# Five plain gate and up pairs for six in a block kernel on one core

## The chip, the cores and the metric

The kernel runs on one core of a Trainium2 chip. The metric is the device time of one launch in microseconds, the median of three runs.

## What is computed

A transformer block on x of 512 tokens by 2048 channels, in float32: a mixer of two head groups (forgetting attention and a gated linear recurrence), and behind it a gated feed-forward part of 6144 hidden channels with a short causal convolution.

```
def conv_gated_mlp(h, w_gate, w_up, conv_ffn_w, conv_ffn_b, w_down):
    g = causal_dwconv(h @ w_gate, conv_ffn_w, conv_ffn_b)
    return (jax.nn.gelu(g) * (h @ w_up)) @ w_down
...
        x = x + rmsnorm(y, norm_mix_post[l])
        h = rmsnorm(x, norm_ffn_pre[l])
        y = conv_gated_mlp(h, w_gate[l], w_up[l], conv_ffn_w[l], conv_ffn_b[l], w_down[l])
        x = x + rmsnorm(y, norm_ffn_post[l])
```

## The kernel before

Data lies channel-major: tiles of 128 channels by 512 tokens. Each float32 operand of a matmul is taken as a high part, rounded to fp32r by ScalarE, and a low part, the rest, formed by VectorE; a product is three matmuls (high by high, high by low, low by high). A matmul here always has 128 x 128 weights and 256 columns.

The feed-forward part has 48 hidden tiles (`FT`), each a gate tile and an up tile that give one tile of h; I call them a pair. The first `PLAIN` = 6 pairs are done plainly. A half tile is one unit of weights (128 x 1024): 8 channel tiles by 2 halves of the tokens by 3 matmuls, 48 in all, and a pair has four units. The first two pairs are computed together, in units 0 to 7, channel tile by channel tile as x1 becomes ready; units 8 to 23 then follow two by two with `tile`. The other `NS` = 42 pairs are done with seven products in place of eight, in the manner of Strassen. A fast product has 24 matmuls. Its right operands are quadrants of the activations (P00, P01, P10, P11, in act_hi and act_lo) and the sums T0 to T3, in tsum. Its left operands are A11, S2, S1, S3, A12, S4 and A22, made from the four weight units of a pair: S1 and S3 by a load with a second, accumulating load on the POOL queue behind it (L722, L727), S2 and S4 by VectorE.

Units and products are named by number in the text: split u is the split of unit u, counted from N_FF.

All five engines run written-out programs that are kept in step by semaphores, so the order in the code is the order on the chip.

- ScalarE: `split(u, s)` waits until the unit has landed in raw[s] and unit u - 2 is used, and writes the high part (L775). `root(5, ...)` takes the root of the channel sum of x1 squared (L780). `gain_x1(k)` scales two tiles of x1. `t_hi(k)` writes the high part of T for channel tile k (L1063). `last_tap` and `gelu_gate` are the convolution's last tap and the gelu.
- VectorE: `split` (L1226), `invert_root` (a reciprocal, L1237), `gate_in(j)` (bank times rms into gb, L1724), `taps(j)` (L1728, L1730), `up_tile(j)` (h_out = bank times cv, L1769), `t_form(k)` (four instructions, L1795 to L1799, into sq), `t_lo(k)` (L1804). T for the down projection is made from h: after an odd pair `t_of_pair(m)` (L1744 to L1747), after the next even one `t3_of_pair(m)` (L1755). sq is the one buffer of `t_form`, so t_form(k + 1) waits for t_split of k.
- SP: loads unit u once split u - 2 is done (L508). Behind the last plain unit it loads for the first fast pair S1 (L539), A11 (L548, waits for the last but one split), S3's first part (L556, behind it), A12 (L565) and A22.
- POOL queue: the stores of T of pair m (`store_pair(m)`: to_stored is L659, te_stored L661, then L664, L665; `store_t3(m)`: L670) and the accumulating loads `add_to_s1`, `add_to_s3`, in the order of this code:

```
            for j in range(PLAIN - 2):
                store_after(j)
            add_to_s1(0)
            add_to_s3(0)
            store_after(PLAIN - 2)
            add_to_s1(1)
```

`store_after(3)` is `store_pair(1)`, and `t3_of_pair(m)` on VectorE waits for it, as it overwrites half of h_out 1:

```
                dve.wait_ge(to_stored, 16 * m + 16)
                dve.wait_ge(tq_ready, m + 1)
```

TensorE waits for a split ahead of each unit and product, and for all eight t_lo ahead of the fast products. The high part of the first fast product's weights waits for all eight t_form, since its place (w_2) is memory that x1 held.

Of the kernel before, what the change touches and what calls it, by code (L numbers as in the profile page):

```python
# [29 lines left out]
P = 128  # L30
# [19 lines left out]
U_OUT = U_MIX + PER_PAIR * NP  # L50
U_FF = U_OUT + 2 * KT
U_DOWN = U_FF + 4 * FT
PLAIN = 6
NS = FT - PLAIN
U_FAST = U_FF + 4 * PLAIN
U_HID = U_FAST + 7 * NS
# [114 lines left out]
def block_kernel(nc, xT, par_d, weights, gate_w, out):  # L171
# [5 lines left out]
    with ExitStack() as ctx:  # L177
# [232 lines left out]
        def t_free_after(c, n):  # L410
# [7 lines left out]
        t2_flat = tsum_f32[:, 2].rearrange("p a k n -> p (a k n)")  # L418
        Y_TILES = [gb[:, 0:S], cv[:], up[:], sq[:, 0]] + [t2_flat[:, S * t:S * t + S] for t in range(8)] + [
            h_out[:, 0], h_out[:, 1], y_rest[:], rms[:]]  # L420
        ADD_BANKS = (banks[2], banks[3], banks[4], banks[5], banks[7], banks[6])
        Y_STAGE = ((rms[:], y_rest[:]), (h_out[:, 0], h_out[:, 1]))


# [345 lines left out]
        def _(act):  # L770
            def split(u, s, more=MORE):

                act.wait_ge(raw_landed[s], (u - s) * 8 + (16 + more[s]))
                at_least(act, unit_used, u - 1)
                act.activation(w_hi[s], k_tiles(raw[:, s]), ACT.Copy).then_inc(hi_done, 1)  # L775

            def root(n, bank, dst, width=D):

                act.wait_ge(sum_done, n)
                act.activation(dst, bank[:], ACT.Sqrt, scale=1.0 / width, bias=eps[:, 0:1]).then_inc(std_done, 1)  # L780
# [296 lines left out]
            gain_x1(2)  # L1077
            gain_x1(3)
            split(N_FF + 11, 1)
            root(5, SB[2], std)  # L1080
            gain_x1(4)
            split(N_FF + 12, 0)
            last_tap(0)
            gain_x1(5)
            split(N_FF + 13, 1)
            gelu_gate(0)
            last_tap(1)
            split(N_FF + 14, 0)
            gelu_gate(1)
            t_hi(0)  # L1090
            last_tap(2)
            split(N_FF + 15, 1)
            gelu_gate(2)
            gain_x1(6)
            last_tap(3)
            split(N_FF + 16, 0)
            t_hi(1)
            gelu_gate(3)
            gain_x1(7)
            split(N_FF + 17, 1)  # L1100
            t_hi(2)
            split(N_FF + 18, 0)
            t_hi(3)
            split(N_FF + 19, 1)
            last_tap(4)
            t_hi(4)
            split(N_FF + 20, 0)
            t_hi(5)
            gelu_gate(4)
            split(N_FF + 21, 1)  # L1110
            t_hi(6)
            split(N_FF + 22, 0)
            t_hi(7)
            split(N_FF + 23, 1)

            def product_hi(i, n):

# [102 lines left out]
        def _(dve):  # L1220
# [585 lines left out]
            def open_used(j, part):  # L1806
                return N_FF + (OPEN if j < 2 else 4 * j + 2 + 2 * part)

            split(N_FF + 11, 1)
            invert_root(5, rms[:], std, 4)  # L1810
            dve.scalar_tensor_tensor(out=acc[:], in0=std, scalar=EPS * D / P, in1=std, op0=ALU.mult, op1=ALU.mult)
            chain(dve.memset(gb[:, 0:2], 0.0))
            split(N_FF + 12, 0)
            gate_in(0, SB[0], open_used(0, 0))
            taps(0)
            split(N_FF + 13, 1)
            up_tile(0, SB[1], open_used(0, 1))
            t_after(0)
            gate_in(1, PT[0], open_used(1, 0))
            t_form(0)  # L1820
            taps(1)
            split(N_FF + 14, 0)
            up_tile(1, PT[1], open_used(1, 1))
            t_after(1)
            gate_in(2, PJ[0], open_used(2, 0))
            t_lo(0)
            taps(2)
            split(N_FF + 15, 1)
            up_tile(2, PJ[1], open_used(2, 1))
            t_after(2)  # L1830
            gate_in(3, PT[2], open_used(3, 0))
            t_form(1)
            taps(3)
            split(N_FF + 16, 0)
            t_lo(1)
            t_form(2)
            split(N_FF + 17, 1)
            up_tile(3, SB[2], open_used(3, 1))
            t_after(3)
            t_lo(2)  # L1840
            t_form(3)
            split(N_FF + 18, 0)
            t_lo(3)
            t_form(4)
            split(N_FF + 19, 1)
            gate_in(4, PJ[0], open_used(4, 0))
            t_lo(4)
            t_form(5)
            taps(4)
            split(N_FF + 20, 0)  # L1850
            t_lo(5)
            t_form(6)
            split(N_FF + 21, 1)
            up_tile(4, PJ[1], open_used(4, 1))
            t_after(4)
            t_lo(6)
            t_form(7)
            split(N_FF + 22, 0)
            t_lo(7)
            split(N_FF + 23, 1)  # L1860

            def product_lo(i, n):

# [147 lines left out]
                at_least(dve, yacc_added, k)  # L2011
                dve.tensor_tensor(acc[:], acc[:], sq[:, 1], ALU.add).then_inc(yacc_added, 1)

            gate_in(PLAIN - 1, PT[0], N_FAST - 2)
            form_s2(0)
            lo(0, 0)
            taps(PLAIN - 1)
# [1 line left out]
            for i in range(NF):  # L2019
                j = PLAIN + i  # L2020
                square = 2 * (i - 1 - NS - 2 * PAIRS_OUT)
                if i:
                    c21_of(i - 1)
                lo(i, 2)
                if i == NS + 1:
                    t_after(FT)
                if square >= 0:
                    add_y_square(square)
                if 0 < i <= NS:
                    taps(j - 1)  # L2030
                lo(i, 3)
                first_of_b(i)
                form_s4(i)
                lo(i, 4)
                if i == 0:
                    up_tile(PLAIN - 1, PT[1], N_FAST)
                elif i <= NS:
                    fast_h(j - 1, i - 1)
                if i <= NS:
                    t_after(j - 1)  # L2040
                if square >= 0:
                    add_y_square(square + 1)
# [39 lines left out]
        def _(pe):  # L2082
# [355 lines left out]
            tile(N_FF + 16, PJ[0])  # L2438
            pe.wait_ge(h_done, 3)
            tile(N_FF + 18, PJ[1])  # L2440
            pe.wait_ge(gate_taken, 2)
            tile(N_FF + 20, PT[0])
            pe.wait_ge(h_done, 2)
            tile(N_FF + 22, PT[1])

            def fast_product(i, n, region, start):

# [29 lines left out]
                else:  # L2477
                    unsplit_product(i, n, region, start)

            pe.wait_ge(t_split, UK)  # L2480
            for i in range(NF):
                a, b, c = [bank[:, 0:HS] for bank in banks[2 + 3 * (i % 2):5 + 3 * (i % 2)]]
                if i > 1:
                    pe.wait_ge(c11_taken, i - 1)
                else:
                    pe.wait_ge(gate_taken, (1, PLAIN)[i])
                one_product(i, 0, a, True)
                if i > 1:
# [109 lines left out]
```

## Time and profile before

| what | value |
|---|---|
| median of three runs | 2143.8 us (2143.32 to 2144.41) |
| the profiled execution | 2143.2 us |
| its span in the trace | 2141.4 us |
| TensorE (PE) busy | 2124.1 us, 99% |
| VectorE (DVE) busy | 1684.1 us, 79% |
| ScalarE (ACT) busy | 1023.3 us, 48% |
| TensorE's granted clock | 0.999 of full speed |

Busy times are sums over the whole span. Matmuls overlap one another and their ends are modelled, so TensorE's work is read from the starts and counts of its matmuls, not from busy time.

### The profile page before, as it was taken

What the parts mean: (1) busy time and instruction counts of PE and PEld (TensorE: products, weight loads), DVE (VectorE), ACT (ScalarE), POOL (GpSimd) and SP (SyncE); (2) the same over time, 40 slices, a digit from 0 to 9 for tenths busy, and PEclk for the clock granted to TensorE, in tenths of its full rate; (3) what the DMA queues carried; (4) which work ended last, traced back from release to release, by engine and by line L of the source; (5) the groups of instructions that cost most, each with busy time, mean ns of one, the idle gap of its engine ahead of it and who ended that gap; (6) DMA issues with size and microseconds to landing.
All of it is one profiled execution on the core that took longest, in us unless ns stands there. A gap on an engine that the chain in (4) does not pass through costs nothing.

```text
span 2141.4 us, 44252 instructions
## 1 busy us (share of the span) xinstructions
PE 2124.1 (99%) x18238; PEld 2093.2 (98%) x18238; DVE 1684.1 (79%) x2297; ACT 1023.3 (48%) x1287; POOL 342.5 (16%) x428
## 2 busy tenths in 40 slices
PE   9999999999999999999999999999999999999998
PEld 8999999999999999999999999999999999999997
DVE  7777777778855877888888888888887867767876
ACT  6555554456322554444444444444444545445543
POOL 0222222222100001212112121121211001012002
PEclk9999999999999999999999999999999999999999
DMA  5788988888543435887887878788888658679645
GB/s 178 163 195 208 209 190 204 200 186 193 155 130 99 153 112 171 233 217 212 220 217 220 225 208 221 214 224 222 230 219 277 193 155 290 177 190 278 204 138 187
DMA packets 238754, 423.84 MB, mean 198 GB/s; under 512 B 17008, under 2 KB 151792, under 8 KB 237312
## 3 DMA queue, kind: packets, MB, share of 16 engines
q1 hardware_dynamic: 147776, 256.84, 36.2%
q0 software_dynamic: 88224, 159.97, 36.0%
q10 hardware_dynamic: 2592, 4.72, 0.6%
q8 instruction: 120, 1.97, 0.4%
q14 instruction: 42, 0.34, 0.0%
HBM read 382.64 MB, written 89.16 MB: 220 GB/s over the span
## 4 chain that ended last, share of the span: by engine, by line
PE 93%; DVE 3%; issue 1%; ACT 1%; DMA 1%; POOL 1%; POOLq 0%; DVEq 0%; ACTq 0%
PE bank L2086 29%; PE bank L2088 29%; PE bank L2087 29%; PE bank L2470 2%; PE bank L2165 1%; PE bank L2178 1%; DVE w_all L1226 1%; DMA act_lo_f<-t_spill 1%; PE bank L2190 0%; PE bank L2189 0%; ACT act_hi L1144 0%; ACT w_all L775 0%; PE bank L2250 0%; DMA t_spill<-h_out 0%; DVE tsum L1804 0%
## 5 line engine op out<-in xcount | busy, mean ns | idle before, releaser
L2086 PE MATMUL bank<-act_hi,w_all 128*128 128x256 f32 x3272 | 909.9, 278 | 5.2 <-DVE w_all L1226 2.5
L2088 PE MATMUL bank<-act_hi,w_all 128*128 128x256 f32 x3272 | 903.9, 276 | 0.0
L2087 PE MATMUL bank<-act_lo,w_all 128*128 128x256 f32 x3272 | 903.8, 276 | 0.0
L2086 PEld LDWEIGHTS bank<-act_hi,w_all 128*128 128x128 f32 x3272 | 614.2, 188 | 11.4 <-issue 4.0
L2087 PEld LDWEIGHTS bank<-act_lo,w_all 128*128 128x128 f32 x3272 | 614.3, 188 | 0.7 <-issue 0.2
L2088 PEld LDWEIGHTS bank<-act_hi,w_all 128*128 128x128 f32 x3272 | 614.3, 188 | 0.0
L2086 PE MATMUL bank<-tsum,w_all 128*128 128x256 f32 x1280 | 353.5, 276 | 0.0
L2088 PE MATMUL bank<-tsum,w_all 128*128 128x256 f32 x1280 | 353.3, 276 | 0.0
L2087 PE MATMUL bank<-tsum,w_all 128*128 128x256 f32 x1280 | 353.3, 276 | 0.0
L1138 ACT ACTIVATE w_all<-raw_s 128x1024 fp32r<-128x1024 f32 x172 | 182.9, 1063 | 242.8 <-PE bank L2088 222.1
L1226 DVE TENSOR_TENSOR w_all<-raw,w_all 128x1024 fp32r<-128x1024 f32 x134 | 164.1, 1225 | 133.6 <-ACT w_all L775 131.9
L1869 DVE TENSOR_TENSOR w_all<-raw_s,w_all 128x1024 fp32r<-128x1024 f32 x172 | 210.6, 1225 | 68.9 <-ACT w_all L1138 67.6
L2087 PEld LDWEIGHTS bank<-tsum,w_all 128*128 128x128 f32 x1280 | 240.2, 188 | 0.0
L2086 PEld LDWEIGHTS bank<-tsum,w_all 128*128 128x128 f32 x1280 | 240.2, 188 | 0.0
L2088 PEld LDWEIGHTS bank<-tsum,w_all 128*128 128x128 f32 x1280 | 240.2, 188 | 0.0
L775 ACT ACTIVATE w_all<-raw 128x1024 fp32r<-128x1024 f32 x133 | 140.7, 1058 | 159.1 <-PE bank L2088 156.8
L2086 PE MATMUL bank<-tsum,w 128*128 128x256 f32 x656 | 181.7, 277 | 0.2 <-DVE pu L1942 0.2
L2087 PE MATMUL bank<-tsum,w 128*128 128x256 f32 x656 | 181.2, 276 | 0.0
L2088 PE MATMUL bank<-tsum,w 128*128 128x256 f32 x656 | 181.1, 276 | 0.0
L2086 PE MATMUL bank<-act_hi,w 128*128 128x256 f32 x568 | 157.3, 277 | 0.0
L2088 PE MATMUL bank<-act_hi,w 128*128 128x256 f32 x568 | 156.8, 276 | 0.0
L2087 PE MATMUL bank<-act_lo,w 128*128 128x256 f32 x568 | 156.8, 276 | 0.0
(401 smaller groups left out, 3524.2 us busy)
## 6 DMA issues: line engine op xcount, KB each, us to landing
raw<-weights SPq DMA_DIRECT2D x262, 512.0 KB, 4.2
w_sums<-weights POOLq DMA_DIRECT2D x96, 512.0 KB, 6.9
raw_s<-weights SPq DMA_DIRECT2D x84, 512.0 KB, 5.4
raw_s<-weights POOLq DMA_DIRECT2D x84, 512.0 KB, 5.7
raw_a<-weights SPq DMA_DIRECT2D x66, 512.0 KB, 5.6
raw_s<-w_sums SPq DMA_DIRECT2D x48, 512.0 KB, 5.2
t_spill<-h_out POOLq DMA_DIRECT2D x48, 256.0 KB, 3.7
act_lo_f<-t_spill POOLq DMA_DIRECT2D x11, 1024.0 KB, 10.0
```

Of the source, the lines that this page charges most:

```text
L775: act.activation(w_hi[s], k_tiles(raw[:, s]), ACT.Copy).then_inc(hi_done, 1)
L1138: act.activation(w_slot(q)[0], k_tiles(RAW_OF[n](i)), ACT.Copy).then_inc(hi_done, 1)
L1226: dve.tensor_tensor(w_lo[s], k_tiles(raw[:, s]), word(w_hi[s]), ALU.subtract).then_inc(split_done, 1)
L1869: dve.tensor_tensor(lo, k_tiles(RAW_OF[n](i)), word(hi), ALU.subtract).then_inc(split_done, 1)
L2086: pe.matmul(dst, ah, bh, start=start, stop=False, skip_group_check=goes_on)
L2087: pe.matmul(dst, ah, bl, start=False, stop=False, skip_group_check=goes_on)
L2088: return pe.matmul(dst, al, bh, start=False, stop=stop, skip_group_check=goes_on)
L2165: last[e] = pe.matmul(dst, q, k, start=t == 0, stop=t == 2)
L2178: last = pe.transpose(dst, sm[:, c:c + P], ident[:])
L2470: last = pe.matmul(region, w[:, k // 2, k % 2], summed[:, k], start=start and k == 0, stop=k == UK - 1, skip_group_check=not start)
```

## The change

`PLAIN` is 5 in place of 6, so the plain pairs end with unit 19 and there are 43 fast pairs. The last plain pair is now number 4, in PJ[0] and PJ[1], handled at the start of the fast loop (gate_in, taps, up_tile). In the opening T 0 and T 1 are formed ahead of the reciprocal, splits, T steps and convolution steps are reordered, the root is written to acc instead of sq, and t3_of_pair(1), which stood behind up_tile(4) and ahead of t_lo(6), stands between t_lo(6) and t_form(7), ahead of up_tile(4). The wait for t_split stands behind the first fast product. The lines that name `PLAIN` elsewhere aren't in the diff, but change with it: the POOL code above now runs store_after(0 to 2), the two additions, store_after(3).

```
-PLAIN = 6
+PLAIN = 5
...
-        ADD_BANKS = (banks[2], banks[3], banks[4], banks[5], banks[7], banks[6])
+        ADD_BANKS = (banks[5], banks[6], banks[7], banks[2], banks[4], banks[3])
...
             split(N_FF + 11, 1)
-            root(5, SB[2], std)
+            t_hi(0)
+            split(N_FF + 12, 0)
+            root(5, SB[2], acc[:])
             gain_x1(4)
-            split(N_FF + 12, 0)
-            last_tap(0)
+            t_hi(1)
             gain_x1(5)
             split(N_FF + 13, 1)
+            last_tap(0)
+            split(N_FF + 14, 0)
             gelu_gate(0)
+            t_hi(2)
...
             def gate_in(j, bank, used):
                 dve.wait_ge(unit_used, used)
+                at_least(dve, conv_done, j)
...
             split(N_FF + 11, 1)
-            invert_root(5, rms[:], std, 4)
-            dve.scalar_tensor_tensor(out=acc[:], in0=std, scalar=EPS * D / P, in1=std, op0=ALU.mult, op1=ALU.mult)
+            t_form(0)
+            t_lo(0)
+            t_form(1)
+            split(N_FF + 12, 0)
+            invert_root(5, rms[:], acc[:], 4)
             chain(dve.memset(gb[:, 0:2], 0.0))
...
             split(N_FF + 18, 0)
-            t_lo(3)
-            t_form(4)
-            split(N_FF + 19, 1)
-            gate_in(4, PJ[0], open_used(4, 0))
             t_lo(4)
             t_form(5)
-            taps(4)
-            split(N_FF + 20, 0)
+            split(N_FF + 19, 1)
             t_lo(5)
             t_form(6)
-            split(N_FF + 21, 1)
-            up_tile(4, PJ[1], open_used(4, 1))
-            t_after(4)
             t_lo(6)
+            t3_of_pair(1)
             t_form(7)
-            split(N_FF + 22, 0)
             t_lo(7)
-            split(N_FF + 23, 1)
+            dve.scalar_tensor_tensor(out=acc[:], in0=acc[:], scalar=EPS * D / P, in1=acc[:], op0=ALU.mult, op1=ALU.mult)
...
-            gate_in(PLAIN - 1, PT[0], N_FAST - 2)
+            gate_in(PLAIN - 1, PJ[0], N_FAST - 2)
...
-                if i <= NS:
+                if 0 < i <= NS:
                     t_after(j - 1)
...
-            pe.wait_ge(gate_taken, 2)
-            tile(N_FF + 20, PT[0])
-            pe.wait_ge(h_done, 2)
-            tile(N_FF + 22, PT[1])
...
-            pe.wait_ge(t_split, UK)
             for i in range(NF):
...
+                if i == 0:
+                    pe.wait_ge(t_split, UK)
                 one_product(i, 1, b, True)
```

**VectorE around the reciprocal.** Before, from split 11 (L1226) to the taps of pair 0:

```order
L1226 TENSOR_TENSOR w_all<-raw,w_all 128x4x2x128
L1237 RECIPROCAL rms<-sq 128x512
L1811 SCALAR_TENSOR_TENSOR acc<-sq 128x512
L1812 MEMSET gb 128x2
L1226 TENSOR_TENSOR w_all<-raw,w_all 128x4x2x128
L1724 TENSOR_TENSOR gb<-bank,rms 128x512
L1728 SCALAR_TENSOR_TENSOR cv<-gb,par,cv 128x512
L1730 SCALAR_TENSOR_TENSOR cv<-gb,par,cv 128x512
```

With the change, where line numbers are 5 or 6 lower (L1220 is the split, L1231 the reciprocal, L1790 to L1794 form T, L1799 its low part):

```order
L1220 TENSOR_TENSOR w_all<-raw,w_all 128x4x2x128
L1790 TENSOR_TENSOR sq<-x 128x256
L1791 TENSOR_TENSOR sq<-x 128x256
L1792 SCALAR_TENSOR_TENSOR sq<-x,sq 128x256
L1794 SCALAR_TENSOR_TENSOR sq<-sq,x 128x256
L1799 TENSOR_TENSOR tsum<-sq,tsum 128x4x256
L1790 TENSOR_TENSOR sq<-x 128x256
L1791 TENSOR_TENSOR sq<-x 128x256
L1792 SCALAR_TENSOR_TENSOR sq<-x,sq 128x256
L1794 SCALAR_TENSOR_TENSOR sq<-sq,x 128x256
L1220 TENSOR_TENSOR w_all<-raw,w_all 128x4x2x128
L1231 RECIPROCAL rms<-acc 128x512
```

Two T steps and one low part moved ahead of the reciprocal, and split 12 too.

**VectorE at the end of the plain pairs.** Before, from t_lo(6) to split 23, gate_in(5), S2 and the low part of the first fast product (L1879, L1869), with the taps behind it:

```order
L1804 TENSOR_TENSOR tsum<-sq,tsum 128x4x256
L1795 TENSOR_TENSOR sq<-x 128x256
L1796 TENSOR_TENSOR sq<-x 128x256
L1797 SCALAR_TENSOR_TENSOR sq<-x,sq 128x256
L1799 SCALAR_TENSOR_TENSOR sq<-sq,x 128x256
L1226 TENSOR_TENSOR w_all<-raw,w_all 128x4x2x128
L1804 TENSOR_TENSOR tsum<-sq,tsum 128x4x256
L1226 TENSOR_TENSOR w_all<-raw,w_all 128x4x2x128
L1724 TENSOR_TENSOR gb<-bank,rms 128x512
L1879 TENSOR_TENSOR raw_s<-raw_s,raw 128x1024
L1869 TENSOR_TENSOR w<-raw,w 128x1024
```

With the change, from t_lo(6) over t3_of_pair(1) (L1750), t_form(7), t_lo(7), the moved acc (L1848) and gate_in(4) (L1719) to S2 (L1867) and the low part of the first fast product (L1857):

```order
L1799 TENSOR_TENSOR tsum<-sq,tsum 128x4x256
L1750 SCALAR_TENSOR_TENSOR h_out<-pu,h_out 128x256
L1790 TENSOR_TENSOR sq<-x 128x256
L1791 TENSOR_TENSOR sq<-x 128x256
L1792 SCALAR_TENSOR_TENSOR sq<-x,sq 128x256
L1794 SCALAR_TENSOR_TENSOR sq<-sq,x 128x256
L1799 TENSOR_TENSOR tsum<-sq,tsum 128x4x256
L1848 SCALAR_TENSOR_TENSOR acc<-acc 128x512
L1719 TENSOR_TENSOR gb<-bank,rms 128x512
L1867 TENSOR_TENSOR raw_s<-raw_s,raw 128x1024
L1857 TENSOR_TENSOR w<-raw,w 128x1024
```

t3_of_pair(1) now stands ahead of T 7, and between T 7 and the first fast product no split of a plain unit is left.

**The POOL queue, from the end of the stores of pair 0 on.** Before, with buffer numbers (the first two rows end T of pair 0, L659 to L665 are pair 1, then come the accumulating loads and store_t3(1)):

```order
L665 DMA t_spill<-pu 128x256
L670 DMA t_spill<-h_out 128x256
L659 DMA t_spill<-h_out 128x2x256
L661 DMA t_spill<-h_out 128x2x256
L664 DMA t_spill<-p1 128x256
L665 DMA t_spill<-pu 128x256
L722 DMA raw_s1<-weights 128x1024
L727 DMA raw_s3<-weights 128x1024
L670 DMA t_spill<-h_out 128x256
L722 DMA raw_s1<-weights 128x1024
```

With the change, with the same line numbers:

```order
L665 DMA t_spill<-pu 128x256
L670 DMA t_spill<-h_out 128x256
L722 DMA raw_s1<-weights 128x1024
L727 DMA raw_s3<-weights 128x1024
L659 DMA t_spill<-h_out 128x2x256
L661 DMA t_spill<-h_out 128x2x256
L664 DMA t_spill<-p1 128x256
L665 DMA t_spill<-pu 128x256
L722 DMA raw_s1<-weights 128x1024
L670 DMA t_spill<-h_out 128x256
```

The two accumulating loads of the first fast pair (L722, L727) moved from behind the four stores of pair 1 (L659 to L665) to ahead of them.

## Rows read from the trace of the kernel before

**Rows 1.** The page: the span, and busy time by engine
```profile
span 2141.4 us, 44252 instructions
...
PE 2124.1 (99%) x18238; PEld 2093.2 (98%) x18238; DVE 1684.1 (79%) x2297; ACT 1023.3 (48%) x1287; POOL 342.5 (16%) x428
```

**Rows 2.** Busy time by stretch: PE, PEld, DVE, ACT, POOL, PEclk, DMA share, GB/s
```profile
900.00:1600.00 700.00, 700.00 (x6179) 700.00 (x6178) 599.69 (x771) 329.27 (x368) 122.33 (x165) 1.00 0.82 220
```

**Rows 3.** TensorE's timeline: start us, us, what [idle before it, releaser]
```profile
768.73 0.28 PE L2086 MATMUL bank<-act_hi,w_all 128*128 128x256 f32 x1
...
775.14 0.28 PE L2087 MATMUL bank<-act_lo,w_all 128*128 128x256 f32 x1
...
805.36 0.36 PE L2086 MATMUL bank<-act_hi,w_all 128*128 128x256 f32 x1 [0.94 <-DVE w_all L1226]
...
849.47 0.28 PE L2086 MATMUL bank<-act_hi,w 128*128 128x256 f32 x1
```

**Rows 4.** VectorE's timeline, 770 to 836
```profile
770.08 1.23 DVE L1226 TENSOR_TENSOR w_all<-raw,w_all 128x1024 fp32r<-128x1024 f32 x1 [0.64 <-ACT w_all L775]
775.95 3.35 DVE L1237 RECIPROCAL rms<-sq 128x512 f32<-128x512 f32 x1 [4.64 <-ACT sq L780]
...
792.36 0.68 DVE L1769 TENSOR_TENSOR h_out<-bank,cv 128x512 f32<-128x512 f32 x1
793.08 0.42 DVE L1744 TENSOR_TENSOR p<-h_out 128x256 f32<-128x256 f32 x1
...
794.22 0.68 DVE L1724 TENSOR_TENSOR gb<-bank,rms 128x512 f32<-128x512 f32 x1
...
799.41 0.69 DVE L1769 TENSOR_TENSOR h_out<-bank,cv 128x512 f32<-128x512 f32 x1 [0.79 <-DMA t_spill<-h_out]
800.02 0.41 DVE L1755 SCALAR_TENSOR_TENSOR h_out<-pu,h_out 128x256 f32<-128x256 f32 x1
800.35 0.68 DVE L1724 TENSOR_TENSOR gb<-bank,rms 128x512 f32<-128x512 f32 x1
800.95 0.42 DVE L1795 TENSOR_TENSOR sq<-x 128x256 f32<-128x256 f32 x1
...
802.54 0.74 DVE L1728 SCALAR_TENSOR_TENSOR cv<-gb,par,cv 128x512 f32<-128x512 f32 x1
...
803.99 1.22 DVE L1226 TENSOR_TENSOR w_all<-raw,w_all 128x1024 fp32r<-128x1024 f32 x1
805.13 1.22 DVE L1804 TENSOR_TENSOR tsum<-sq,tsum 128x1024 fp32r<-128x1024 f32 x1
...
835.32 1.22 DVE L1226 TENSOR_TENSOR w_all<-raw,w_all 128x1024 fp32r<-128x1024 f32 x1
```

**Rows 5.** ScalarE's timeline, the high part of T for one k
```profile
808.16 1.07 ACT L1063 ACTIVATE tsum<-sq 128x1024 fp32r<-128x1024 f32 x1 [1.24 <-DVE sq L1799]
```

**Rows 6.** Timeline of the POOL queue's DMA issues near 842
```profile
842.42 0.87 POOL L727 DMA_DIRECT2D raw_s<-weights  x1 [4.58 <-DMA raw_s<-weights]
842.98 0.88 POOL L670 DMA_DIRECT2D t_spill<-h_out  x1
```

**Rows 7.** DMA issues of 793.3 to 793.4, last column us to landing
```profile
t_spill<-h_out POOLq DMA_DIRECT2D x1, 256.0 KB, 3.6
```

**Rows 8.** DMA issues of 842.9 to 843.0
```profile
raw_s<-weights POOLq DMA_DIRECT2D x1, 512.0 KB, 8.9
t_spill<-h_out POOLq DMA_DIRECT2D x1, 128.0 KB, 9.1
```

**Rows 9.** DMA issues of 800.7 to 800.8
```profile
t_spill<-h_out POOLq DMA_DIRECT2D x1, 128.0 KB, 2.2
```

**Rows 10.** Busy time by stretch, 707 to 713, columns as in rows 2
```profile
707.00:709.00 2.00, 1.72 (x15) 1.63 (x15) 1.67 (x3) 1.25 (x3) 0.00 (x0) 1.00 0.00 0
709.00:711.00 2.00, 1.84 (x7) 1.38 (x6) 0.91 (x4) 0.00 (x0) 0.00 (x0) 0.55 0.41 105
711.00:713.00 2.00, 2.00 (x4) 0.69 (x3) 1.72 (x5) 0.51 (x1) 0.00 (x0) 0.60 0.46 161
```

More of the change, by code:

```diff
@@ L1079, in _ @@
             split(N_FF + 11, 1)
-            root(5, SB[2], std)
+            t_hi(0)
+            split(N_FF + 12, 0)
+            root(5, SB[2], acc[:])
             gain_x1(4)
-            split(N_FF + 12, 0)
-            last_tap(0)
+            t_hi(1)
             gain_x1(5)
             split(N_FF + 13, 1)
+            last_tap(0)
+            split(N_FF + 14, 0)
             gelu_gate(0)
+            t_hi(2)
             last_tap(1)
-            split(N_FF + 14, 0)
+            split(N_FF + 15, 1)
             gelu_gate(1)
-            t_hi(0)
             last_tap(2)
-            split(N_FF + 15, 1)
+            gain_x1(6)
+            split(N_FF + 16, 0)
             gelu_gate(2)
-            gain_x1(6)
             last_tap(3)
-            split(N_FF + 16, 0)
-            t_hi(1)
+            split(N_FF + 17, 1)
+            t_hi(3)
             gelu_gate(3)
             gain_x1(7)
-            split(N_FF + 17, 1)
-            t_hi(2)
             split(N_FF + 18, 0)
-            t_hi(3)
+            t_hi(4)
             split(N_FF + 19, 1)
-            last_tap(4)
-            t_hi(4)
-            split(N_FF + 20, 0)
             t_hi(5)
-            gelu_gate(4)
-            split(N_FF + 21, 1)
             t_hi(6)
-            split(N_FF + 22, 0)
             t_hi(7)
-            split(N_FF + 23, 1)
             def product_hi(i, n):
@@ L1809, in _ @@
             split(N_FF + 11, 1)
-            invert_root(5, rms[:], std, 4)
-            dve.scalar_tensor_tensor(out=acc[:], in0=std, scalar=EPS * D / P, in1=std, op0=ALU.mult, op1=ALU.mult)
+            t_form(0)
[3 more added lines that the diff above has]
+            invert_root(5, rms[:], acc[:], 4)
             chain(dve.memset(gb[:, 0:2], 0.0))
-            split(N_FF + 12, 0)
             gate_in(0, SB[0], open_used(0, 0))
+            split(N_FF + 13, 1)
@@ L1815, in _ @@
             taps(0)
-            split(N_FF + 13, 1)
+            t_lo(1)
+            gate_in(1, PT[0], open_used(1, 0))
+            t_form(2)
+            split(N_FF + 14, 0)
             up_tile(0, SB[1], open_used(0, 1))
             t_after(0)
-            gate_in(1, PT[0], open_used(1, 0))
-            t_form(0)
+            t_lo(2)
             taps(1)
-            split(N_FF + 14, 0)
+            split(N_FF + 15, 1)
+            gate_in(2, PJ[0], open_used(2, 0))
             up_tile(1, PT[1], open_used(1, 1))
@@ L1824, in _ @@
             t_after(1)
-            gate_in(2, PJ[0], open_used(2, 0))
-            t_lo(0)
             taps(2)
-            split(N_FF + 15, 1)
+            split(N_FF + 16, 0)
+            gate_in(3, PT[2], open_used(3, 0))
             up_tile(2, PJ[1], open_used(2, 1))
             t_after(2)
-            gate_in(3, PT[2], open_used(3, 0))
-            t_form(1)
+            t_form(3)
             taps(3)
-            split(N_FF + 16, 0)
-            t_lo(1)
-            t_form(2)
             split(N_FF + 17, 1)
+            t_lo(3)
@@ L1838, in _ @@
             up_tile(3, SB[2], open_used(3, 1))
             t_after(3)
-            t_lo(2)
-            t_form(3)
+            t_form(4)
             split(N_FF + 18, 0)
-            t_lo(3)
-            t_form(4)
-            split(N_FF + 19, 1)
-            gate_in(4, PJ[0], open_used(4, 0))
             t_lo(4)
             t_form(5)
-            taps(4)
-            split(N_FF + 20, 0)
+            split(N_FF + 19, 1)
             t_lo(5)
             t_form(6)
-            split(N_FF + 21, 1)
@@ L1854, in _ @@
-            up_tile(4, PJ[1], open_used(4, 1))
-            t_after(4)
             t_lo(6)
+            t3_of_pair(1)
             t_form(7)
-            split(N_FF + 22, 0)
             t_lo(7)
-            split(N_FF + 23, 1)
+            dve.scalar_tensor_tensor(out=acc[:], in0=acc[:], scalar=EPS * D / P, in1=acc[:], op0=ALU.mult, op1=ALU.mult)
             def product_lo(i, n):
@@ L2035, in _ @@
                 if i == 0:
-                    up_tile(PLAIN - 1, PT[1], N_FAST)
+                    up_tile(PLAIN - 1, PJ[1], N_FAST)
                 elif i <= NS:
                     fast_h(j - 1, i - 1)
-                if i <= NS:
+                if 0 < i <= NS:
                     t_after(j - 1)
@@ L2485, in _ @@
                 else:
-                    pe.wait_ge(gate_taken, (1, PLAIN)[i])
+                    pe.wait_ge(gate_taken, (1, 2)[i])
                 one_product(i, 0, a, True)
@@ L2490, in _ @@
                 else:
-                    pe.wait_ge(h_done, (1, PLAIN)[i])
+                    pe.wait_ge(h_done, (1, 2)[i])
+                if i == 0:
+                    pe.wait_ge(t_split, UK)
                 one_product(i, 1, b, True)
```

## The prediction

> **What bounds the kernel now.** I read the page first. TensorE is busy for 2124.1 of 2141.4 us [rows 1], so only two things can shorten the run: fewer matmuls, or shorter holes between them. One number prices the matmuls. Between 900 and 1600 us, 6179 of them start in 700 us, 0.1133 us each, at a granted clock of 1.00 [rows 2]. A half tile of a plain pair (I call it a unit) is 48 matmuls, 5.44 us; a product of a fast pair is 24, 2.72 us.
>
> Next I read TensorE's timeline where plain pairs end and fast ones begin, because the diff acts there. Count units from the first gate and up weights, so that the change's last plain unit is 19 and the present one's is 23. Unit 10 starts at 768.73 and unit 11's second matmul at 775.14. The first fast product starts at 849.47 [rows 3]. From 775.14 to there are 13 units less one matmul, 623 x 0.1133 = 70.6 us, but 74.3 us pass. So 3.7 us are holes; the row at 805.36 is the largest of them, and the releaser is VectorE's low part of a weight split (L1226) [rows 3]. TensorE waits for VectorE here.
>
> Last I read VectorE's timeline for what each step costs, from one start to the next [rows 4]: split 1.14 (803.99 to 805.13), forming T for one k 1.60 (four instructions, 800.95 to 802.54), its low part 1.14 (the same shape as a split), gate 0.60, up 0.60, both taps 1.45, reciprocal about 3.4, t_of_pair 1.13, t3_of_pair 0.33. A T buffer is reused: T of k+1 waits until the low part of k is done, and the low part waits for ScalarE's high part, 1.07 us [rows 5]. A T step with nothing to fill that wait is about 4.1 us. Before the reciprocal VectorE is idle for 4.64 us [rows 4].
>
> **Part by part.**
>
> *Matmuls.* One plain pair (192) becomes a fast one (168): 24 x 0.1133 = 2.7 us less. The fast stage is one pair longer, 168 x 0.1133 = 19.03 us, and may start 19.03 us earlier than now before anything is lost. Break-even for the first fast product is therefore 849.47 - 19.03 = 830.4.
>
> *TensorE until then.* Unit 10 starts at 768.73. Ten units are 54.4 us; the two matmuls of the channel sum add about 0.9 us (unit 11's first matmuls, 775.14 - 768.73 - 5.44). If no split is late, the plain part ends at 824.0, so the change could bring at most 6.4 us.
>
> *VectorE, same stretch.* It keeps all eight T steps but loses 21.8 us in which to do them. Start at 771.23, after split 11 [rows 4]. T 0, its low part and T 1 go into the idle time ahead of the reciprocal. Up to the end of split 18 it issues: reciprocal and memset 3.5, seven splits 8.0, five T 8.0, four low parts 4.6, four gates 2.4, four ups 2.4, four taps 5.8, two t_of_pair 2.3, one t3 0.3: 37.3 us. To these I add 4.0 us of waits: 1.3 for the high part of T 0, 1.6 in up 2 for the store of pair 0 (it goes 7.05 us after up 1 now, 792.36 to 799.41, and up 1 falls at 794.5), and about 1.1 of small ones. Split 18 starts at 811.4 and is done at 812.6. All splits of units 12 to 19 come out 0.2 us or more ahead of TensorE, so the present holes go. Then follow, with little beside them: low 4, T 5, split 19, low 5, T 6, low 6, and VectorE stands before t3_of_pair(1) at 822.0. That is 9.4 us later, of which 1.3 is the wait for high part 6.
>
> *The moved wait.* t3_of_pair(1) overwrites half of h_out 1, so it waits for to_stored(1), the store of pair 1 on the POOL queue. This store is moved too, by the loop bound PLAIN - 2: it stood ahead of the two accumulating weight loads and now stands behind both. The POOL queue can't issue it before L727, and L727 waits for raw_s3, which SP loads only after the split of the last unit but one. Now: that split starts at 835.32 [rows 4], L727 issues at 842.42, 7.1 us later, and the next DMA of the queue at 842.98 [rows 6]. After: 811.4 + 7.1 = 818.5, and the store issues at 819.0.
>
> How long does it take to land? No row shows this store behind L727, so I bound it. Alone on the queue, the same store took 3.6 us [rows 7], giving 822.6. The DMA that now stands right behind L727 (L670, half the size) took 9.1 us, where L727 itself took 8.9 [rows 8] and L670 alone took 2.2 [rows 9]. It landed 0.8 us after L727 did. I take 9.1: the same five weight transfers surround it, all some 24.5 us earlier. Store landed: 828.1.
>
> The Trainium skill, page DMA: Bandwidth & Descriptors, section on the anatomy of one DMA on the gpsimd path, gives a fit of 2.0 us plus bytes over 436 GB/s; for 256 KB that is an estimate of 2.6 us, and the sum would then end near +1.3 us. The row behind L727 is more than three times as long, and I go by it.
>
> *From there to the first fast product.* t3 0.35; T 7 1.67; its high part 1.10; low part 1.18; the moved acc 0.64; gate 4 0.60; sum S2 1.14 (same shape as a split); low part of product 0 1.22; 0.06 to TensorE: 8.0 us in series. Queued behind the waiting instruction are all of these, and TensorE waits for the last. First fast product: 836.1. Low part 1 follows 2.6 us later, just inside product 0's 2.72.
>
> *The clock.* TensorE is then idle from 824.0 to 836.1. After the sparse work before 709 (15 matmuls in 2 us) the granted clock averages 0.55 over 709 to 711 and 0.60 over 711 to 713 [rows 10]; at 0.5 or 1 that is 1.8 and 1.6 us at the lower level, 3.4 together. If it is at 1.2 instead of 2.4 GHz for 3.4 us of the fast stage, half of that is lost: 1.7 us. Bounds: nothing, if it rises at once, and 3.4 us if it stays down twice as long.
>
> *Nothing for:* root written into acc, swapped banks of the last adds, gate_in's wait for conv_done (the taps always stand ahead), and the later stage, which is shifted as it is. Cover for the last: VectorE is busy 599.7 of 700 us there [rows 2].
>
> **Sum.** 836.1 - 830.4 = +5.7; clock +1.7; together +7.4 us on the profiled 2143.2, or 2150.6. The median of the runs shown is 0.6 above that execution: 2151.2.
>
> **Rivals.**
> 1. *The store isn't held up* (it lands 3 to 5.5 us after issue). Then VectorE is the limit: 822.0 + 8.0 = 830.0, 0.4 under break-even, with the clock +1.3; with 5.5 us for the store +3.8. Time 2145.1 to 2147.6. For it: alone it took 3.6. Against: the weight loads in flight beside it. The fit of the Trainium skill's page, above, would put it here.
> 2. *It is faster*: VectorE's series is shorter than I lay it out, so that the fast stage starts at 824.0 to 826 and the 2.7 and 3.7 us are kept. Time 2137.4 to 2139.5. It decides only if the store is landed and VectorE is at t3_of_pair(1) by 818, 1 us before the queue can even issue the store, so I give it little.
> 3. *The clock does not fall, or falls for longer.* 2149.5, or 2152.9. Idle TensorE is what speaks for a fall; that it was not quite idle at 707 leaves the size open.
> 4. *A second late thing in the first fast pair*, such as S3 or the sums' weights behind the same queue: +2 to +4 on top, up to 2155.
>
> **How the numbers follow.** About 0.2% (4.3 us) is what a measurement of this kernel tells from no change. Forecast with its clock variants 0.70; rival 1 0.17; rival 2 0.05; rival 4 0.08. Of rival 1 all is within 4.3 us; of the forecast about 0.05 is (store in 7 us, no clock loss). So faster 0.05, same 0.22, slower 0.73. The range 2145.5 to 2154 leaves out rival 2, the low end of rival 1 and the top of rival 4; for the likeliest case alone it is 2148.5 to 2153.
>
> **What the profile after would show.** Units 12 to 19 without a hole, ending near 824. One hole on TensorE of about 12 us before the first fast product. In VectorE's timeline an idle time of about 6 us before a t3_of_pair, released by the DMA of t_spill from h_out. L659 issued just behind L727 near 819. A lower clock for some 3.4 us. I am wrong if that wait is absent or under 1 us, if the splits are late in units 16 to 19, or if holes appear in the fast stage that aren't there now.

## The result, and the profile after

The changed kernel takes 2152.14 us (median of 7 runs, 2149.17 to 2152.96), the kernel before 2143.32 us (7 runs, 2142.89 to 2144.41). The ratio is 1.0037, with a 95% interval of 1.0028 to 1.0046. It is slower by 8.8 us, where 7.4 were forecast. Two of the seven runs took 2149.2 and 2149.4 us at a mean granted clock of 0.997, the other five 2151.7 to 2153.0 at 0.995 or 0.996; one of the five was profiled, and what makes the two shorter is not known. The profiled execution took 2152.96 us, 9.8 more than the one of before, and its rows are compared with rows 1 to 10.

The page's first line and its line of busy times:

```profile
span 2151.2 us, 44227 instructions
...
PE 2123.5 (99%) x18214; PEld 2093.0 (97%) x18214; DVE 1691.9 (79%) x2308; ACT 1024.2 (48%) x1291; POOL 344.2 (16%) x430
```

The span grew by 9.8 us [rows 1] while TensorE's busy time fell by 0.6: what was added is waiting. TensorE's waits say for whom, longest first (us in total, times, longest):

```profile
PE bank L2074 <- DVE w L1857: 11.7, 1, 11.7
...
PE bank L2074 <- DVE up L1938: 1.4, 1, 1.4
PE bank L2454 <- DVE pu L1930: 1.4, 1, 1.4
```

One wait of 11.7 us is new, for L1857, the low part of a fast product's weights. The wait for up was 1.4 us before too, the one for pu 0.6. The timeline of TensorE at that place, the rows that answer to [rows 3]:

```profile
769.26 0.28 PE L2074 MATMUL bank<-act_hi,w_all 128*128 128x256 f32 x1
...
775.68 0.28 PE L2075 MATMUL bank<-act_lo,w_all 128*128 128x256 f32 x1
...
824.45 0.28 PE L2076 MATMUL bank<-act_hi,w_all 128*128 128x256 f32 x1
836.42 0.55 PE L2074 MATMUL bank<-act_hi,w 128*128 128x256 f32 x1 [11.70 <-DVE w L1857]
```

The last plain unit ends at 824.45, and the first fast product starts at 836.42. From 775.68 on there is no hole before that: the present holes, 3.7 us, are gone. VectorE's timeline over the same time [rows 4]:

```profile
820.31 1.22 DVE L1799 TENSOR_TENSOR tsum<-sq,tsum 128x1024 fp32r<-128x1024 f32 x1 [1.13 <-ACT tsum L1063]
828.44 0.43 DVE L1750 SCALAR_TENSOR_TENSOR h_out<-pu,h_out 128x256 f32<-128x256 f32 x1 [6.91 <-DMA t_spill<-h_out]
828.78 0.42 DVE L1790 TENSOR_TENSOR sq<-x 128x256 f32<-128x256 f32 x1
...
831.58 1.23 DVE L1799 TENSOR_TENSOR tsum<-sq,tsum 128x1024 fp32r<-128x1024 f32 x1 [1.12 <-ACT tsum L1063]
832.72 0.68 DVE L1848 SCALAR_TENSOR_TENSOR acc<-acc 128x512 f32<-128x512 f32 x1
833.32 0.68 DVE L1719 TENSOR_TENSOR gb<-bank,rms 128x512 f32<-128x512 f32 x1
833.92 1.22 DVE L1867 TENSOR_TENSOR raw_s<-raw_s,raw 128x1024 f32<-128x1024 f32 x1
835.06 1.22 DVE L1857 TENSOR_TENSOR w<-raw,w 128x1024 fp32r<-128x1024 f32 x1
```

VectorE ends the low part of T 6, then stands for 6.91 us before L1750, which is t3_of_pair(1), and the releaser is the DMA of t_spill from h_out. Behind it come, in series, T 7, its low part, the moved acc, gate 4, S2 and the low part of the first product. The POOL queue and the landings of its DMAs [rows 6, 8]:

```profile
820.47 0.87 POOL L727 DMA_DIRECT2D raw_s<-weights  x1 [8.44 <-DMA raw_s<-weights]
821.06 1.03 POOL L659 DMA_DIRECT2D t_spill<-h_out  x1
```

```profile
raw_s<-weights POOLq DMA_DIRECT2D x1, 512.0 KB, 7.1
t_spill<-h_out POOLq DMA_DIRECT2D x1, 256.0 KB, 7.4
```

The store of pair 1 (L659) is issued just behind L727 and takes 7.4 us to land, so it lands near 828.5; VectorE goes on at 828.44. The same store took 3.6 alone [rows 7]. Last the clock, in the columns of [rows 2]:

```profile
820.00:824.40 4.40, 4.40 (x41) 4.40 (x40) 1.22 (x1) 0.27 (x1) 3.45 (x5) 1.00 0.99 306
824.40:827.20 2.80, 0.32 (x3) 0.12 (x2) 0.00 (x0) 0.00 (x0) 0.89 (x1) 1.00 1.03 274
827.20:836.40 9.20, 0.00 (x0) 0.01 (x1) 6.77 (x11) 4.04 (x5) 0.56 (x1) 0.50 0.51 112
836.40:840.80 4.40, 4.38 (x20) 4.40 (x21) 3.56 (x4) 0.78 (x1) 0.00 (x0) 0.50 0.45 123
840.80:844.80 4.00, 4.00 (x37) 4.00 (x36) 1.69 (x3) 1.84 (x3) 0.00 (x0) 0.99 0.00 0
```

TensorE stood still from the end of its last matmul, started at 824.45, and from 827.2 on its granted clock is 0.50, also for the first 4.4 us of fast products: 20 matmuls there, 37 in the 4.0 us behind. The first fast product lasts from 836.42 to 841.31, 4.9 us in place of 2.7.

### The profile page after: what moved, and what is told of

It reads as the page before. It is cut to its first block, busy times and chain, and to the rows that moved or that the text cites. A ratio compares the mean times of both kernels' runs of the same rounds, so it can differ in the third digit from the quotient of the medians.

```text
span 2151.2 us, 44227 instructions
## 1 busy us (share of the span) xinstructions
PE 2123.5 (99%) x18214; PEld 2093.0 (97%) x18214; DVE 1691.9 (79%) x2308; ACT 1024.2 (48%) x1291; POOL 344.2 (16%) x430
## 4 chain that ended last, share of the span: by engine, by line
PE 91%; DVE 3%; DMA 2%; ACT 1%; issue 1%; POOL 1%; POOLq 0%; DVEq 0%; SPq 0%; ACTq 0%
PE bank L2074 29%; PE bank L2075 29%; PE bank L2076 29%; PE bank L2454 1%; DMA raw<-weights 1%; PE bank L2153 1%; PE bank L2166 1%; DMA act_lo_f<-t_spill 1%; PE bank L2178 0%; PE bank L2177 0%; ACT act_hi L1138 0%; ACT w_all L775 0%; DMA raw_s<-weights 0%; DMA t_spill<-h_out 0%; DVE w_all L1220 0%
## 5 line engine op out<-in xcount | busy, mean ns | idle before, releaser
L2074 PE MATMUL bank<-act_hi,w_all 128*128 128x256 f32 x3216 | 893.6, 278 | 0.4 <-DVE act_lo L1225 0.2
L2076 PE MATMUL bank<-act_hi,w_all 128*128 128x256 f32 x3216 | 888.5, 276 | 0.0
L2075 PE MATMUL bank<-act_lo,w_all 128*128 128x256 f32 x3216 | 888.5, 276 | 0.0
L2074 PEld LDWEIGHTS bank<-act_hi,w_all 128*128 128x128 f32 x3216 | 604.0, 188 | 5.0 <-issue 2.2
L2075 PEld LDWEIGHTS bank<-act_lo,w_all 128*128 128x128 f32 x3216 | 604.0, 188 | 0.7 <-issue 0.2
L2076 PEld LDWEIGHTS bank<-act_hi,w_all 128*128 128x128 f32 x3216 | 603.9, 188 | 0.0
L2074 PE MATMUL bank<-tsum,w_all 128*128 128x256 f32 x1312 | 362.8, 277 | 0.9 <-DVE cv L1956 0.6
L2076 PE MATMUL bank<-tsum,w_all 128*128 128x256 f32 x1312 | 362.1, 276 | 0.0
L2075 PE MATMUL bank<-tsum,w_all 128*128 128x256 f32 x1312 | 362.1, 276 | 0.0
L1857 DVE TENSOR_TENSOR w_all<-raw_s,w_all 128x1024 fp32r<-128x1024 f32 x176 | 215.4, 1224 | 71.7 <-ACT w_all L1132 70.4
L1220 DVE TENSOR_TENSOR w_all<-raw,w_all 128x1024 fp32r<-128x1024 f32 x130 | 159.2, 1224 | 131.5 <-ACT w_all L775 129.8
L2074 PEld LDWEIGHTS bank<-tsum,w_all 128*128 128x128 f32 x1312 | 246.3, 188 | 1.6 <-DVE cv L1956 1.0
L2075 PEld LDWEIGHTS bank<-tsum,w_all 128*128 128x128 f32 x1312 | 246.3, 188 | 0.1
L2076 PEld LDWEIGHTS bank<-tsum,w_all 128*128 128x128 f32 x1312 | 246.2, 188 | 0.0
L2074 PE MATMUL bank<-act_hi,w 128*128 128x256 f32 x584 | 163.5, 280 | 13.8 <-DVE w L1857 11.7
L2075 PE MATMUL bank<-act_lo,w 128*128 128x256 f32 x584 | 162.3, 278 | 0.0
L2076 PE MATMUL bank<-act_hi,w 128*128 128x256 f32 x584 | 162.2, 278 | 0.0
```

The source lines that it names most:

```text
L1220: dve.tensor_tensor(w_lo[s], k_tiles(raw[:, s]), word(w_hi[s]), ALU.subtract).then_inc(split_done, 1)
L1857: dve.tensor_tensor(lo, k_tiles(RAW_OF[n](i)), word(hi), ALU.subtract).then_inc(split_done, 1)
L2074: pe.matmul(dst, ah, bh, start=start, stop=False, skip_group_check=goes_on)
L2075: pe.matmul(dst, ah, bl, start=False, stop=False, skip_group_check=goes_on)
L2076: return pe.matmul(dst, al, bh, start=False, stop=stop, skip_group_check=goes_on)
```

## Experiments

All comparisons are with the runs of the kernel before on the same chip (medians of 2143.39 for the first four, 2143.27 for the last two). Differences from the changed kernel are differences of medians from separate sets of runs.

**Stores first.** On the POOL queue the stores of pair 1 go back ahead of the two accumulating loads.

```
-            for j in range(PLAIN - 2):
+            for j in range(PLAIN - 1):
                 store_after(j)
             add_to_s1(0)
             add_to_s3(0)
-            store_after(PLAIN - 2)
```

> The changed kernel, with the stores of T of pair 1 put back ahead of the two accumulating loads on the POOL queue; nothing else differs. Theory (the moved store makes VectorE wait in t3_of_pair(1)): the idle time of 6.91 us before that instruction goes, the first fast product starts 7.0 us earlier in the trace (836.4 to about 829.5), TensorE's hole shrinks from 12.0 to about 5, and since TensorE still idles, a stretch at the lower clock may stay, worth 0 to 2.5 us. Time 2143 to 2146, against 2152.1 of the changed kernel. Rival (VectorE has too much to do in the shorter opening, and the wait only stands where it would be late anyway): the hole stays above 9 us and the time above 2149.

Measured 2145.87 us (11 runs, 2144.54 to 2147.31), ratio 1.0011 (1.0002 to 1.0020): 6.3 us less than the changed kernel. In its timeline of the POOL queue the store is issued 13.6 us sooner, and in VectorE's the wait is gone:

```profile
807.47 0.72 POOL L659 DMA_DIRECT2D t_spill<-h_out  x1 [5.37 <-DVE h_out L1763]
...
820.25 0.88 POOL L727 DMA_DIRECT2D raw_s<-weights  x1 [8.53 <-DMA raw_s<-weights]
```

```profile
820.00 1.23 DVE L1798 TENSOR_TENSOR tsum<-sq,tsum 128x1024 fp32r<-128x1024 f32 x1 [1.13 <-ACT tsum L1062]
821.14 0.42 DVE L1749 SCALAR_TENSOR_TENSOR h_out<-pu,h_out 128x256 f32<-128x256 f32 x1
...
824.28 1.22 DVE L1798 TENSOR_TENSOR tsum<-sq,tsum 128x1024 fp32r<-128x1024 f32 x1 [1.13 <-ACT tsum L1062]
...
827.76 1.22 DVE L1856 TENSOR_TENSOR w<-raw,w 128x1024 fp32r<-128x1024 f32 x1
```

t3_of_pair(1) (L1749) follows the low part of T 6 by 1.14 us. TensorE's hole, in its timeline, is 824.14 to 829.12:

```profile
824.14 0.28 PE L2075 MATMUL bank<-act_hi,w_all 128*128 128x256 f32 x1
829.12 0.55 PE L2073 MATMUL bank<-act_hi,w 128*128 128x256 f32 x1 [4.71 <-DVE w L1856]
```

So 7 us of the hole of 12 hung on the place of four stores in one queue. The other 5 are VectorE's own line; whether they are its amount of work or its order, this run can't tell (the two-buffer kernel below does).

**t3 later.** The POOL queue stays as in the change; VectorE takes t3_of_pair(1) later.

```
             t_lo(6)
-            t3_of_pair(1)
             t_form(7)
...
             taps(PLAIN - 1)
             lo(0, 1)
+            t3_of_pair(1)
+            dve.wait_ge(t3_ready, 2)
```

The last line waits for the end of t3_of_pair(1) itself.

> The changed kernel, with t3_of_pair(1) on VectorE moved from ahead of T 7 to behind the low part of the second fast product; the order of the POOL queue is that of the changed kernel, so the store is as late as there. Theory (it is the waiting instruction in VectorE's line, not the DMA traffic, that costs): the same as with the store put first, hole about 4.7 us, time 2143 to 2146, within 1 us of that kernel, though the store still lands near 828. Rival (the late store or its traffic delays the first fast pair in some other way): a wait turns up behind it and the time stays above 2149.

Measured 2144.96 us (11 runs, 2143.97 to 2146.42), ratio 1.0006 (0.9997 to 1.0015). The store is as late as in the changed kernel, issued at 820.61 and 7.0 us on its way, but t3_of_pair(1) (L1750) now stands at 831.65, behind the landing:

```profile
820.31 1.22 DVE L1799 TENSOR_TENSOR tsum<-sq,tsum 128x1024 fp32r<-128x1024 f32 x1 [1.13 <-ACT tsum L1063]
...
824.45 1.23 DVE L1799 TENSOR_TENSOR tsum<-sq,tsum 128x1024 fp32r<-128x1024 f32 x1 [1.13 <-ACT tsum L1063]
...
827.93 1.22 DVE L1856 TENSOR_TENSOR w<-raw,w 128x1024 fp32r<-128x1024 f32 x1
...
831.65 0.42 DVE L1750 SCALAR_TENSOR_TENSOR h_out<-pu,h_out 128x256 f32<-128x256 f32 x1
```

```profile
t_spill<-h_out POOLq DMA_DIRECT2D x1, 256.0 KB, 7.0
```

The first fast product starts at 829.30, as with the stores first (829.12), though the store is late. So it was the waiting instruction in VectorE's line that made the late store cost time; the traffic costs nothing that shows. The two cures are 0.9 us apart, within the 1 us expected.

**Busy TensorE.** In the changed kernel, between the last plain unit and the first fast product:

```
+            pe.wait_ge(gate_taken, 2)
+            pe.wait_ge(h_done, 2)
+            keep_busy(50, PT[1])
             for i in range(NF):
```

> The changed kernel, with 50 matmuls of 128 columns on a free bank put between the last plain unit and the first fast product, about 10.7 us of TensorE work in a hole of 12.0 us; their results are used by nothing. Theory (the idle hole lowers the clock and the first fast product pays for it): the granted clock stays at 1.00, the first fast product takes 2.7 in place of 4.9 us and starts where it did (836.4), time 2.2 us below the changed kernel, 2149.9. Rival (the low clock costs nothing, since the fast pair that follows waits for VectorE anyway): the time stays within 0.5 us of 2152.1.

Measured 2149.42 us (8 runs, 2148.89 to 2152.58), ratio 1.0027 (1.0017 to 1.0038): 2.7 us below the changed kernel's median. The profiled run is its slowest, with everything from unit 10 on 1.3 us later, but the clock is plain in it. Windows of 4 us, TensorE alone (busy, matmuls, clock, DMA share, GB/s), and TensorE's timeline at the hole:

```profile
828.00:832.00 4.00, 4.00 (x38) 1.00 1.05 242
832.00:836.00 4.00, 4.00 (x38) 1.00 0.17 48
836.00:840.00 4.00, 3.59 (x31) 1.00 0.38 109
```

```profile
825.88 11.32 PE L2238 MATMUL bank<-ones 128*128 128x128 f32 x100
837.62 0.35 PE L2074 MATMUL bank<-act_hi,w 128*128 128x256 f32 x1 [0.41 <-DVE w L1857]
840.53 0.28 PE L2074 MATMUL bank<-tsum,w_all 128*128 128x256 f32 x1
```

The clock is 1.00 throughout. The first fast product still waits for VectorE at the end of the filling matmuls and starts at 837.62, within 0.1 us of 836.42 and those 1.3 us. It lasts 2.9 us in place of 4.9. That the lower clock is what made it long rests on this trace. The times agree with it but don't prove it: the intervals of the two ratios (1.0028 to 1.0046 and 1.0017 to 1.0038) overlap, and by the means of the runs (2151.5 and 2149.7) the gain is 1.8 us in place of 2.7.

**Six pairs in the new order.** The kernel before with all of the change's reordering up to split 19 on VectorE and ScalarE (T 0, its low part, T 1 and split 12 ahead of the reciprocal, root in acc), and pair 4 kept; only the part behind split 19 is new. VectorE's part of the edit, against the changed kernel (ScalarE's line gets back its steps of pair 4 and splits 20 to 23):

```
             split(N_FF + 19, 1)
+            gate_in(4, PJ[0], open_used(4, 0))
             t_lo(5)
             t_form(6)
+            taps(4)
+            split(N_FF + 20, 0)
             t_lo(6)
-            t3_of_pair(1)
             t_form(7)
+            split(N_FF + 21, 1)
+            up_tile(4, PJ[1], open_used(4, 1))
+            t_after(4)
             t_lo(7)
...
+            split(N_FF + 22, 0)
+            split(N_FF + 23, 1)
```

> The kernel before with its six plain pairs, in which VectorE and ScalarE take the changed kernel's order: T 0 and T 1 ahead of the reciprocal, splits as they come free, T sums sooner; the low part of T 7 stands ahead of split 22. Theory (the reordering alone takes the 3.7 us of holes out, and all of the loss comes from the shortened opening): no hole between unit 11 and the first fast product, time 2139.6, 3.7 us below 2143.3. Rival (the reordering itself costs, for example by making a split late): 2143 or more, with a hole in units 16 to 23.

Measured 2140.23 us (11 runs, 2139.26 to 2141.10), ratio 0.9986 (0.9977 to 0.9995), 3.2 us below before. Between 770 and 860 us TensorE waits for nothing in its trace, and the first fast product starts at 846.48, where it was 849.47:

```profile
846.48 0.28 PE L2087 MATMUL bank<-act_hi,w 128*128 128x256 f32 x1
```

The reordering half of the change is a gain by itself.

**Two buffers for T.** Stores first, and the series behind T shortened.

```
+        def t_buffer(k):
+            if k in (5, 7):
+                return raw_s24[:].rearrange("p (b n) -> p b n", n=HS)
+            return sq[:].rearrange("p a (b n) -> p (a b) n", n=HS)
...
             t_form(4)
+            t_form(5)
             split(N_FF + 18, 0)
             t_lo(4)
-            t_form(5)
-            split(N_FF + 19, 1)
-            t_lo(5)
             t_form(6)
+            t_lo(5)
+            split(N_FF + 19, 1)
+            t_form(7)
             t_lo(6)
             t3_of_pair(1)
-            t_form(7)
             t_lo(7)
-            dve.scalar_tensor_tensor(out=acc[:], ...)
...
-            gate_in(PLAIN - 1, PJ[0], N_FAST - 2)
-            form_s2(0)
             lo(0, 0)
-            taps(PLAIN - 1)
+            dve.wait_ge(t_split, UK)
+            form_s2(0)
+            dve.scalar_tensor_tensor(out=acc[:], ...)
+            gate_in(PLAIN - 1, PJ[0], N_FAST - 2)
             lo(0, 1)
+            taps(PLAIN - 1)
```

`t_form(k)` now waits for the low part that last used its own buffer, not for that of k - 1. On ScalarE t_hi(5) goes ahead of split 19, and the high part of product 1 ahead of the last tap of pair 4.

> Five plain pairs, the stores of pair 1 first, and the series behind T shortened: T 5 and T 7 are formed in raw_s24, free by then, so that T of one k no longer waits for the low part of the one before it; the low part of the first fast product stands ahead of S2, the moved acc and gate 4, and taps 4 behind the low part of the second. Theory (what is left of the hole, 5.0 us, is the series of T steps with nothing beside them, plus 3 us of work that the first product doesn't need): laid out by durations, the low part of product 0 is done at about 823.6 and TensorE needs it at 824.4, so no hole and no stretch at the lower clock; against the kernel with the stores first 5.0 - 0.1 and 2.3 us less: 2138.7 from 2145.9. Rival (VectorE's total work in the shorter opening is the limit, in whatever order): a hole of 2 us or more stays, time above 2141.

Measured 2137.63 us (8 runs, 2137.17 to 2139.04), ratio 0.9974 (0.9964 to 0.9985): 5.6 us below before, 14.5 below the changed kernel's median and 1.1 below the 2138.7 expected. (The wait for cv late in the kernel, 1.2 us with the stores first, is absent from this trace.) VectorE's timeline to the low part of the first product (L1865), and TensorE's at the seam:

```profile
818.28 0.42 DVE L1799 TENSOR_TENSOR raw_s<-x 128x256 f32<-128x256 f32 x1
...
819.88 1.22 DVE L1808 TENSOR_TENSOR tsum<-sq,tsum 128x1024 fp32r<-128x1024 f32 x1
821.01 0.42 DVE L1755 SCALAR_TENSOR_TENSOR h_out<-pu,h_out 128x256 f32<-128x256 f32 x1
821.35 1.22 DVE L1808 TENSOR_TENSOR tsum<-raw_s,tsum 128x1024 fp32r<-128x1024 f32 x1
822.48 1.22 DVE L1865 TENSOR_TENSOR w<-raw,w 128x1024 fp32r<-128x1024 f32 x1
823.62 1.22 DVE L1875 TENSOR_TENSOR raw_s<-raw_s,raw 128x1024 f32<-128x1024 f32 x1
```

```profile
824.50 0.28 PE L2086 MATMUL bank<-act_hi,w_all 128*128 128x256 f32 x1
824.61 0.28 PE L2084 MATMUL bank<-act_hi,w 128*128 128x256 f32 x1
```

From T 7 on nothing waits: each row starts where the one before lets it. The low part starts at 822.48, lasts 1.22, and is done 0.9 us before TensorE takes it at 824.61, 0.11 behind the matmul before. With the stores first the low part started at 827.76, 6.6 us behind t3_of_pair(1) at 821.14; here it is 1.5 us behind 821.01. Of the 5.1 us between, 2.3 are acc, gate 4 and S2, moved behind it; the rest is T 7, formed ahead of t3_of_pair(1), and the wait of 1.13 for its high part, which is gone. The rival, VectorE's total work, is out as the limit: what the first product needs fits in time once its order is changed. Both edits were made in one kernel, so how much each gives in time alone was not measured. Against the six pairs in the new order it is 2.6 us faster, which is the price of 24 matmuls (2.7).

**Stores first, and busy.** Stores first with `keep_busy(20, PT[1])` at the place of the 50 above.

> Stores of pair 1 first, and 20 matmuls of 128 columns on a free bank in the hole of 5.0 us that is left there; their results are used by nothing. Theory (in that kernel 4.6 us of the first fast products run at the lower clock, worth 2.3 us): the granted clock stays at 1.00 and the time is 2.3 us below its 2145.9, 2143.6, with the first fast product still starting near 829. Rival (a hole of 5 us costs nothing beyond itself): 2145.4 to 2146.4.

Measured 2142.22 us (11 runs, 2141.51 to 2143.99), ratio 0.9994 (0.9985 to 1.0003): 3.7 us below the kernel with the stores first, where 2.3 were expected. The same two windows of 4 us, first of the kernel with the stores first, then of this one (TensorE alone):

```profile
828.00:832.00 4.00, 2.88 (x13) 0.50 0.78 207
832.00:836.00 4.00, 4.00 (x29) 0.74 0.03 10
```

```profile
828.00:832.00 4.00, 3.76 (x33) 1.00 0.67 191
832.00:836.00 4.00, 4.00 (x37) 1.00 0.18 26
```

The low clock is gone. The two profiled executions, 3.3 us apart, can be compared step by step. The first fast product starts at 829.12 and 829.10, so the filling matmuls delayed nothing; the second product starts at 834.26 and 831.92, so the clock gives 2.3 us, as expected. Up to the wait for pu near 1660 us the distance stays 2.4; there the matmuls' starts are 1.72 us apart with the stores first and 0.86 here, which is the other 0.9. So the 1.4 us by which the medians exceed the forecast are not the clock; most of it is the wait for pu, if these executions are typical. Why that wait differs is not shown.

## Why the prediction was right

1. **Matmuls and break-even.** 168 x 0.1133 for the longer fast stage, break-even at 830.4. The six-pair and the two-buffer kernel, both without a hole there, are 2.6 us apart, for 2.7 by the sum.
2. **The present holes go.** Right: none between unit 11 and the end of unit 19, and the six-pair kernel gives 3.2 us for them, where the count in the trace was 3.7.
3. **VectorE's line.** It was laid out to stand before t3_of_pair(1) at 822.0. It did at 821.5, in a run that began this stage 0.5 us later, so the line took 1.0 us less. Up 2 is most of it: a wait of 1.6 us for a store was forecast and none came, since that store landed in 3.2 us where it took 5.2 before. Later waits take 0.6 back.
4. **The moved wait.** The path was right; that the number fits so well is luck, for three errors cancel. Split 18 was forecast for 811.4 and came at 810.31. L727 was to follow it by 7.1 us and followed by 10.2, at 820.47, because the load of S3's first part on SP's queue (L556, issued at 811.94) took 8.2 us, where it took 5.2 before. And the store was to take 9.1 us and took 7.4. Errors of -1.1, +3.1 and -1.7 us give a landing at 828.1 by the sum, 828.4 measured. The premise that the same weight loads surround L727 did not hold: SP's next three were issued 1.2 to 0.3 us ahead of L727 before (841.20 to 842.08), and 4.2 to 3.3 us ahead of it after (816.28 to 817.13). The mechanism doesn't hang on that; it is shown from both sides, by moving the store and by moving the instruction that waits. The estimate of 2.6 us for the store by the Trainium skill's page (DMA: Bandwidth & Descriptors, the anatomy of one DMA on the gpsimd path) is not what this place gives: 7.4 and 7.0 us behind an accumulating load, 3.9 with the stores first.
5. **The series behind it.** 8.0 us from t3_of_pair(1) to the first fast product; 828.44 to 836.42 is 8.0.
6. **The clock.** 1.7 us by the sum, 2.2 in the trace (4.9 for a product of 2.7). The term was mis-sized by 0.5: I took the length of the one stretch at the lower level before, 3.4 us, and the stretch after a true standstill held 4.4 us of fast work. The Trainium skill's page TensorE: Matmul & The Clock Gate (Part 1, What's actually happening) has the clock at the lower rate as the default that activity lifts; the trace agrees, as the clock was still at 0.50 when the matmuls began.

In the profiled run the sum closes: unit 10 began 0.5 us later (769.26 for 768.73), the hole costs 836.42 - 0.53 - 830.44 = 5.5, the clock 2.2, and two waits late in the kernel about 1.6 (for pu, 1.73 for 0.98 us between two matmuls' starts, and for cv, 1.01 for 0.11). Together 9.8.

The last two stand in the stage for which the prediction put nothing, and a hole there that was absent before was one of its signs of being wrong. The one for cv is in four of the six traces with five plain pairs and in neither with six; t3 later and two buffers don't have it, so the change doesn't bring it every time. The one for pu is 1.0 and 1.2 us between the matmuls' starts in the two traces with six plain pairs, 1.6 to 1.9 in five with five plain pairs, and 0.9 in the sixth. Each may come with the change in part; no run separates it, and the cause stays open.

Rival 1 (the store not held up) is what the stores-first kernel makes true, and there the time was 2145.9, inside the 2145.1 to 2147.6 given for it. Rival 2 was to need t3_of_pair(1) by 818; the two-buffer kernel reaches its time, 2137.6, in another way: t3_of_pair(1) is at 821.0 there, and the steps behind it are fewer. Rival 3's two cases, no loss by the clock or 3.4 us, both missed: it was 2.2. Rival 4 did not come: in the trace no two matmuls of the fast stage start over 0.6 us apart before 1614 us.

## What to carry to other kernels

When a loop bound or a stage's length changes, list every queue whose order comes out of it, the DMA queues too: here a bound of `PLAIN - 2` put four small stores behind two large loads, and an instruction in the busiest helper's line waited for them. Lay out the helper engine's series up to the first thing that the bound engine needs, and take out of it what isn't needed for that; the same change loses 8.8 us or gains 5.6 by nothing but the order and one spare buffer. Price a long hole on the bound engine above its length: behind the two looked at here, of 12.0 and 5.0 us, the matmuls ran at half the clock for 4.4 and 5.0 us, which cost 2.2 and 2.3 us more; the holes before the change, of 0.9 us and less each, left the clock at 1.00.

## What the runs showed that I had not expected

- TensorE's clock fell 2.8 us into the standstill (824.4 to 827.2) and came back 4.4 us after the first matmul of the fast stage; in the kernel with the stores first the hole was 5.0 us, and the cost of the lower clock as large, 2.3 us (0.50 from the first fast matmul at 829.1 to 834.1). Filling the hole with matmuls that compute nothing kept the clock at 1.00 both times. The forecast sized this term from the stretch at the lower clock near 709 us [rows 10]; in one trace, of stores first and busy, that stretch stays at 1.00, though the edit doesn't touch it.
- A store right behind an accumulating load of 512 KB on the same queue landed just after that load. In the changed kernel it was 0.9 us after it (7.1 us for the load, 7.4 for the store from its issue 0.6 us later), at twice the 3.6 us of the same store in another place; with t3 later it was 0.8 us after, and the 128 KB store behind L727 before 0.8. No run parts the queue's order from the load of the DMA engines, which were busy at a share of about 1.0 there: that the one queue is the cause is likely, not shown.
